# Splitting the first layer-norm block by tokens and moving the last tile's masks into the next tile

## The chip, the cores and the metric

The kernel runs on one core of one Trainium2 chip. The metric is the device time of one execution in microseconds; the time before is the median of three runs. The profile is of one further execution, with times counted from the start of its span.

## The reference

The reference is one step of a two-layer model on 384 tokens (128 context, 256 latent) of width D = 1024, in float32. Cut to the parts that matter here:

```python
def conv_module(h, pw1, dw, dw_b, ln_g, ln_b, pw2):
    a, g = jnp.split(h @ pw1, 2, axis=-1)
    u = a * jax.nn.sigmoid(g)
    u = depthwise_conv(u, dw) + dw_b            # 31 taps
    u = jax.nn.silu(layer_norm(u, ln_g, ln_b))
    return u @ pw2

def layer_norm(x, g, b):
    xc = x - mean(x)
    return xc * lax.rsqrt(mean(xc * xc) + EPS) * g + b

def moe_swiglu(h, w_router, w1, w3, w2):        # 8 experts, top 2
    out = 0
    for e in range(8):
        out = out + gates[:, e:e + 1] * ((silu(t @ w1[e]) * (t @ w3[e])) @ w2[e])
```

Layer 0 is the convolution module followed by a dense SwiGLU, layer 1 is latent attention followed by the eight experts. Each part is preceded by an RMS norm that a small linear map of the condition modulates.

## The kernel before, in words

Every product with a weight matrix is made in three TensorE passes, high times high, low times high and high times low (`mm3`, lines 277 to 279). So each weight chunk (1 MB, [128, 2048]) passes four stations. SyncE loads it into one of six slots of `raw` (`load`, line 240); ScalarE makes the high part `wh` (`make_hi`, line 255); VectorE makes the low part `wl` = raw − wh (`make_lo`, line 261); TensorE uses both. `wh` and `wl` have three slots each. A slot of `raw` is free once its low part is made, and a slot of `wh` and `wl` once TensorE has used the chunk. The order on each engine is written out by hand, one instruction stream an engine, tied by counting semaphores.

**Start of the convolution.** ScalarE modulates the normed input in eight blocks of 128 channels, and VectorE splits each block into `hTh` and `hTl` (`split_block`, lines 415 and 417). VectorE makes the low part of the first weight chunk, PW1, between the first split and the other seven. TensorE's first product needs that low part and the first split block, and each later one the next block.

**Layer norm of the convolution.** Channels lie on partitions, eight blocks `v[:, j, :]` of 399 columns: 128 context tokens, 15 columns of padding, 256 latent tokens. TensorE sums the squares over all channels with a matrix of ones into PSUM (line 1715). Then, once for all 399 columns: ScalarE takes the root into `sd` (line 749), VectorE the reciprocal `rs` (line 1130). For each block j VectorE scales by `rs` (line 1134), ScalarE applies Silu in two pieces of 128 and 256 tokens (line 753), and VectorE splits the result. Line 1136 splits block j − 2 after scaling block j. TensorE's product with `pw2` (`pw2_block`) waits for the split of block k and takes three groups of 128 tokens from it, of six passes each.

**Experts.** Tokens sorted by expert are handled in tiles of 128. Expert 0's first tile is gathered on the chip by a product with selection masks; its chunks are MOE to MOE+11 (six for w1, six for w3). GpSimd meanwhile writes all tokens to `xs_dram` with six indirect DMAs (line 660), and then makes the masks `selL` of the last tile (lines 667 to 678), which are needed only at the very end of the kernel. In the first tile, after its eighth chunk (MOE+7), TensorE waits for these masks, transposes them and makes six short passes for the gate weights (lines 2116 to 2122). ScalarE then copies `sel` and `selT` (lines 977 to 981) and VectorE copies `slot_w` (lines 1569 to 1573), each in order between two weight conversions.

After MOE+9 TensorE turns the rows of the second tile, `xrow` (line 2100). SyncE fetches them (line 521) when all six indirect DMAs have landed; until then it issues nothing else, since the next chunks stand behind that wait on its queue. The function `tile` then handles the chunks NEXT to NEXT+17 (NEXT = MOE+12) of the next tile: w1 six, w3 six, w2 six chunks. It is written once as a static call, `tile(0, static=True)`, and then runs in a loop.

Of the kernel before, what the change touches and what calls it, by code (L numbers as in the profile page):

```python
# [15 lines left out]
P = 128  # L16
# [37 lines left out]
def hybrid_conv_mla_diffusion_step(nc, d, out):  # L54
# [45 lines left out]
    POST_TAPS = (24, 30, 38)  # L100
    GATE_EARLY = 4
    TILE_CH = 6 * NG
    NEXT = MOE + 12
# [3 lines left out]
    with ctx:  # L107
# [88 lines left out]
        def sem(name):  # L196

            if name not in named:
                named[name] = ctx.enter_context(nc.semaphore(name))
            return named[name]  # L200
# [210 lines left out]

        def split_block(dve, q, made, per, j):

            dve.wait_ge(sem(made), per * (j + 1))
            dve.tensor_copy(hTh[:, j, :], hf[:, j, :]).then_inc(sem("h_hi"), 1)
            dve.wait_ge(sem("h_hi"), SPLITS.index(q) * DK + j + 1)
            dve.tensor_tensor(hTl[:, j, :], hf[:, j, :], hTh[:, j, :], ALU.subtract).then_inc(sem(q + "_h_lo"), 1)  # L417
# [13 lines left out]
        def _(sp):  # L431
# [91 lines left out]
            with sp.Fori(1, NE - 1) as e:  # L523
                load_next(e, e + 1, e)
            sp.wait_ge(sem("tab_ready"), 1)
            more = sp.value_load(tab[0:1, 0:1], min_val=0, max_val=NX)
# [13 lines left out]
        def _(pool):  # L540
# [124 lines left out]
            pool_step.n = 9  # L665
            pool.wait_ge(sem("weights_made"), 1)
            pool_step(pool.tensor_scalar(first, jt[:, 2, NE - 1:NE], float(NE - 1), float(P), ALU.add, ALU.mult))
# [23 lines left out]
        def _(act):  # L691
# [56 lines left out]
            act.wait_ge(sem("ln_summed"), DK)  # L748
            act.activation(sd, ps[:, 5, 0:CV], ACT.Sqrt, scale=1.0 / D, bias=epsc[:, 0:1]).then_inc(sem("ln_root"), 1)
            for j in range(DK):  # L750
                act.wait_ge(sem("ln_scaled"), j + 1)
                for a, b, o in ((0, P, 0), (P, T, SV - P)):
                    act.activation(hf[:, j, a:b], v[:, j, a + o:b + o], ACT.Silu, scale=vT[:, LNG + j:LNG + j + 1],
                                   bias=vT[:, LNB + j:LNB + j + 1]).then_inc(sem("ln_done"), 1)
# [155 lines left out]
            turned_k(0, turns())  # L910
            act.wait_ge(sem("first_turned"), 1)
            act.activation(KR[:, :], ps[:, 3, :], ACT.Copy).then_inc(sem("rT_made"), 1)
# [29 lines left out]
            token_scale(0)  # L942
            act.wait_ge(sem("x_turned"), 1)
            act.activation(yacc[:, 0, :], ps[:, X_BANKS[0]:X_BANKS[0] + 2, :].rearrange("p a b -> p (a b)"),
# [30 lines left out]
            for k in range(2 * UP - 1):  # L975
                make_hi(act, MOE + k + 3)
                if k == UP + 1:
                    act.wait_ge(sem("last_tile"), TC + 1)
                    for c in range(TC):
                        act.activation(sel[:, c, :], ident[:, :], ACT.Copy, scale=rt[:, 9, c, 3:4])  # L980
                    act.activation(selT[:, :], ps[:, 6, 0:T], ACT.Copy).then_inc(sem("last_tile"), 1)
                if k == UP:
                    silu(MOE + UP, None)
                if k == 2 * UP - 3:
                    rows_hi(xgh[:, :, :], (sem("xg_turned"), 1))
# [6 lines left out]
            def tile(e, static=False):  # L992

                L, L1, L3 = (None,) * 3 if static else ((e, TILE_CH), (e, 1), (e, 3))
                for k in range(-1, TILE_CH - 1):
                    make_hi(act, NEXT + k + 3, L)
                    if k in (1, 2, 3):
                        hidden_hi(k - 1, L3)
                    if k == 1 and not static:
                        store_y(ys_dram[ds(e * P - P, P), :], at(1, L1), sem("y_stored"))  # L1000
                    if k == UP:
                        act.wait_ge(sem("hm_made"), at(3, L3))
                        silu(NEXT + UP, L)
                    if k == 2 * UP + 2:
                        rows_hi(xgh[:, :, :], (sem("xg_turned"), at(2, L1)))
                act.wait_ge(chunk_used, at(NEXT + TILE_CH, L))
                if not static:
                    act.wait_ge(sem("y_stored"), at(0, (e, 16)))
                act.activation(ybuf[:, :], ps[:, 6:8, :].rearrange("p a b -> p (a b)"), ACT.Copy).then_inc(sem("y_copied"), 1)

            tile(0, static=True)
            with act.Fori(1, NE - 1) as e:
                tile(e)
            act.wait_ge(sem("tab_ready"), 1)
            more = act.value_load(tab[0:1, 0:1], min_val=0, max_val=NX)
# [14 lines left out]
        def _(dve):  # L1030
# [59 lines left out]
            modulation(0)  # L1090
            split_block(dve, "conv", "conv_modulated", 2, 0)
            make_lo(dve, PW1)
            for j in range(1, DK):
                split_block(dve, "conv", "conv_modulated", 2, j)
            dve.wait_ge(sem("zeroed"), 3)
# [31 lines left out]
            for q in range(2):  # L1127
                make_lo(dve, pw2_chunk(q))
            dve.wait_ge(sem("ln_root"), 1)
            step(dve.reciprocal(rs, sd))  # L1130
            dve.wait_ge(sem("ln_centred"), DK)
            for j in range(DK + 2):
                if j < DK:
                    dve.tensor_tensor(v[:, j, :], v[:, j, :], rs, ALU.mult).then_inc(sem("ln_scaled"), 1)
                if j >= 2:
                    split_block(dve, "ln", "ln_done", 2, j - 2)
            add_bias(4)
# [284 lines left out]
            for c in (1, 2):  # L1422
                dve.wait_ge(sem("x_turned"), c + 1)
                dve.tensor_copy(yacc[:, c, :], ps[:, X_BANKS[c]:X_BANKS[c] + 2, :].rearrange("p a b -> p (a b)")).then_inc(sem("router_made"), 1)
# [86 lines left out]
            def weights():  # L1511

                dve.wait_ge(sem("token_steps"), 3 * TC + 1)
                step(dve.tensor_scalar(gap[:, :, 2:3], gap[:, :, 1:2], 1.0, None, ALU.add))
                dve.reciprocal(gap[:, :, 3:4], gap[:, :, 2:3]).then_inc(sem("weights_made"), 1)

# [44 lines left out]
            for k in range(1, 2 * UP - 1):  # L1561
                if k == 2 * UP - 2:
                    product(MOE + 2 * UP, None, 1, groups=(0,))
                make_lo(dve, MOE + k + 3)
                if k == 2:
                    extra_tiles()
                if k == 4:
                    table()
                if k == UP + 1:
                    dve.wait_ge(sem("last_tile"), TC + 1)  # L1570
                    step(dve.tensor_copy(slot_w[:, :], ps[:, 7, 0:2]))
                    dve.wait_ge(sem("last_tile"), TC + 2)
                    dve.sem_inc(sem("y_copied"), 1)
                if k == 2 * UP - 3:
                    rows_lo(xgl[:, :, :], xgh[:, :, :], 0, (sem("xg_hi"), 1))
            product(MOE + 2 * UP, None, 1, groups=(1,))

            def tile(e, static=False):

                L, L1, L3 = (None,) * 3 if static else ((e, TILE_CH), (e, 1), (e, 3))  # L1580
                for k in range(-1, TILE_CH - 1):
# [3 lines left out]
                    if k in (1, 2, 3):  # L1585
                        hidden_lo(k - 1, L3)
                    if k == 2 * UP:
                        product(NEXT + 2 * UP, L, at(2, L1), (sem("hm_turned"), at(3, L3)))
# [36 lines left out]
        def _(pe):  # L1625
# [94 lines left out]
            def pw2_block(q, i, c, hi, lo):  # L1720

                k = 2 * q + i
                pe.wait_ge(sem("ln_h_lo"), k + 1)
                for h in range(2):
# [4 lines left out]

            pe.wait_ge(sem("ln_root"), 1)  # L1730
            for q in range(DK // 2):
# [273 lines left out]
            for c in range(KC):  # L2005
                last = pe.transpose(ps[:, 3, c * P:(c + 1) * P], krh[:, c, :, :].rearrange("p a b -> p (a b)"), ident[:, :])
            last.then_inc(sem("first_turned"), 1)
            pe.wait_ge(sem("q_copied"), 1)
# [105 lines left out]
            for i in range(UP):  # L2114
                up_chunk(MOE + UP, i, 3, hgh, hgl, None)
                if i == 1:
                    pe.wait_ge(sem("last_tile"), TC)
                    for c in range(TC):
                        pe.transpose(ps[:, 6, c * P:(c + 1) * P], selL[:, c, :], ident[:, :])
                    for c in range(TC):  # L2120
                        last = pe.matmul(ps[:, 7, 0:2], selL[:, c, :], GL[:, c, :], start=c == 0, stop=c == TC - 1)
                    last.then_inc(sem("last_tile"), 1)
                if i == UP - 3:
                    turn_rows_in(1, 16)

            def tile(e, static=False):
# [8 lines left out]
                for i in range(UP):  # L2135
                    up_chunk(NEXT + UP, i, 3, xgh, xgl, L)
                pe.wait_ge(sem("y_copied"), at(1, L1))
                for i in range(2 * NG):
# [5 lines left out]
            with pe.Fori(1, NE - 1) as e:  # L2144
                tile(e)
            pe.wait_ge(sem("tab_ready"), 1)
            more = pe.value_load(tab[0:1, 0:1], min_val=0, max_val=NX)
# [77 lines left out]
```

## Time and profile before

| | |
|---|---|
| runs before, median (lowest to highest) | 1447.17 us (1446.88 to 1450.38) |
| the profiled execution, its own time | 1447.64 us |
| its span | 1445.9 us |
| mean granted TensorE clock | 0.978 of full speed |
| TensorE busy | 1369.8 us, 95% |
| VectorE busy | 1060.7 us, 73% |
| ScalarE busy | 756.3 us, 52% |
| GpSimd busy | 100.6 us, 7% |
| bytes moved by DMA | 351 MB, 243 GB/s over the span |

The execution's own time is 1.7 us above its span and 0.5 us above the median of the runs. Busy times of different engines overlap. In the rows below, PE is TensorE, PEld its weight load, DVE is VectorE, ACT is ScalarE, POOL is GpSimd and SPq SyncE's DMA issues. L1130 is line 1130 of the kernel before.

### The profile page before, as it was taken

What the parts mean: (1) busy time and instruction counts of PE and PEld (TensorE: products, weight loads), DVE (VectorE), ACT (ScalarE), POOL (GpSimd) and SP (SyncE); (2) the same over time, 40 slices, a digit from 0 to 9 for tenths busy, and PEclk for the clock granted to TensorE, in tenths of its full rate; (3) what the DMA queues carried; (4) which work ended last, traced back from release to release, by engine and by line L of the source; (5) the groups of instructions that cost most, each with busy time, mean ns of one, the idle gap of its engine ahead of it and who ended that gap; (6) DMA issues with size and microseconds to landing.
All of it is one profiled execution on the core that took longest, in us unless ns stands there. A gap on an engine that the chain in (4) does not pass through costs nothing.

```text
span 1445.9 us, 18716 instructions
## 1 busy us (share of the span) xinstructions
PE 1369.8 (95%) x6687; PEld 1100.4 (76%) x6687; DVE 1060.7 (73%) x1328; ACT 756.3 (52%) x764; POOL 100.6 (7%) x129
## 2 busy tenths in 40 slices
PE   4999989999999989899999978799999999999997
PEld 1885456999999978677777757587878878878875
DVE  1689985443433457888888889588888888888986
ACT  2431355222312255655555545577777777777773
POOL 2000000401000001100000015200000000000003
PEclk8999999999999989999999998899999999999999
DMA  9898556989743324322222235799999999999994
GB/s 376 293 339 322 204 203 225 400 337 64 198 145 103 122 50 128 104 66 66 79 80 87 89 116 206 301 375 375 363 385 380 364 363 395 369 362 381 385 361 152
DMA packets 91914, 351.17 MB, mean 243 GB/s; under 512 B 7279, under 2 KB 43447, under 8 KB 62679
## 3 DMA queue, kind: packets, MB, share of 16 engines
q1 hardware_dynamic: 81088, 316.95, 61.4%
q0 software_dynamic: 9040, 28.66, 5.8%
q10 hardware_dynamic: 1735, 4.89, 0.8%
q8 instruction: 30, 0.49, 0.1%
q14 instruction: 21, 0.17, 0.0%
HBM read 326.13 MB, written 24.35 MB: 242 GB/s over the span
## 4 chain that ended last, share of the span: by engine, by line
PE 81%; DVE 8%; ACT 3%; issue 3%; POOL 2%; DMA 1%; ACTq 0%; DVEq 0%
PE ps L277 23%; PE ps L279 22%; PE ps L278 22%; PE ps L1699 3%; PE ps L1644 3%; DVE wl L261 2%; DVE hm L1551 2%; PE ps L1945 2%; DMA raw<-in_conv_pw 1%; PE ps L1976 1%; ACT wh L255 1%; PE ps L1949 1%; POOL xs_dram L660 1%; PE ps L2107 1%; ACT QB L850 0%
## 5 line engine op out<-in xcount | busy, mean ns | idle before, releaser
L261 DVE TENSOR_TENSOR wl<-raw,wh 128x2048 fp32r<-128x2048 f32 x253 | 575.9, 2290 | 151.8 <-ACT wh L255 151.6
L255 ACT ACTIVATE wh<-raw 128x2048 fp32r<-128x2048 f32 x253 | 484.1, 1917 | 306.0 <-PE ps L279 267.4
L277 PE MATMUL ps<-wh,xgh 128*128 128x512 f32 x432 | 173.5, 402 | 0.1
L279 PE MATMUL ps<-wh,xgl 128*128 128x512 f32 x432 | 171.1, 396 | 0.0
L278 PE MATMUL ps<-wl,xgh 128*128 128x512 f32 x432 | 171.0, 396 | 0.0
L277 PE MATMUL ps<-hTh,wh 128*128 128x384 f32 x480 | 164.7, 343 | 1.8 <-DVE hTl L417 1.8
L278 PE MATMUL ps<-hTl,wh 128*128 128x384 f32 x480 | 163.3, 340 | 0.0
L279 PE MATMUL ps<-hTh,wl 128*128 128x384 f32 x480 | 163.0, 340 | 0.0
L277 PE MATMUL ps<-wh,hgh 128*128 128x512 f32 x288 | 118.2, 410 | 3.6 <-DVE hgl L1557 1.9
L278 PE MATMUL ps<-wl,hgh 128*128 128x512 f32 x288 | 115.8, 402 | 0.0
L279 PE MATMUL ps<-wh,hgl 128*128 128x512 f32 x288 | 115.6, 402 | 0.0
L1072 DVE SCALAR_TENSOR_TENSOR v<-u,dwT,v 128x399 f32<-128x399 f32 x180 | 99.1, 639 | 0.0
L277 PEld LDWEIGHTS ps<-hTh,wh 128*128 128x128 f32 x480 | 90.5, 189 | 10.8 <-issue 7.9
L1158 DVE TENSOR_TENSOR ff<-ps,fs 128x384 f32<-128x384 f32 x22 | 12.3, 558 | 114.9 <-PE ps L279 114.9
L279 PEld LDWEIGHTS ps<-wh,xgl 128*128 128x128 f32 x432 | 81.4, 188 | 19.8
L277 PEld LDWEIGHTS ps<-wh,xgh 128*128 128x128 f32 x432 | 81.4, 188 | 19.1 <-DVE wl L261 0.4
L278 PEld LDWEIGHTS ps<-wl,xgh 128*128 128x128 f32 x432 | 81.4, 188 | 18.3
L278 PEld LDWEIGHTS ps<-hTl,wh 128*128 128x128 f32 x480 | 90.7, 189 | 0.4
L279 PEld LDWEIGHTS ps<-hTh,wl 128*128 128x128 f32 x480 | 90.6, 189 | 0.0
L277 PEld LDWEIGHTS ps<-wh,hgh 128*128 128x128 f32 x288 | 55.2, 192 | 20.8 <-DVE wl L261 5.5
L279 PEld LDWEIGHTS ps<-wh,hgl 128*128 128x128 f32 x288 | 55.3, 192 | 13.6
L278 PEld LDWEIGHTS ps<-wl,hgh 128*128 128x128 f32 x288 | 55.4, 192 | 12.5
(368 smaller groups left out, 2122.7 us busy)
## 6 DMA issues: line engine op xcount, KB each, us to landing
raw<-in_moe_w SPq DMA_DIRECT2D x180, 1024.0 KB, 6.1
raw<-in_ada_w SPq DMA_DIRECT2D x48, 1024.0 KB, 6.6
raw<-in_ffn_w SPq DMA_DIRECT2D x33, 1024.0 KB, 11.5
raw<-in_conv_pw SPq DMA_DIRECT2D x12, 1024.0 KB, 9.2
raw<-in_mla_wo SPq DMA_DIRECT2D x8, 1024.0 KB, 4.8
xs_dram<-hf POOLq DMA_DIRECT2D x14, 512.0 KB, 21.2
ys_dram<-hf POOLq DMA_DIRECT2D x14, 512.0 KB, 22.3
raw<-in_mla_wuq SPq DMA_DIRECT2D x8, 768.0 KB, 4.6
```

Source lines behind the costliest of these rows:

```text
L255: act.activation(wh[:, split_no(s) % HL, :], raw[:, s % RAW, :], ACT.Copy).then_inc(hi_made, 1)
L261: eng.tensor_tensor(wl[:, split_no(s) % HL, :], raw[:, s % RAW, :], wh[:, split_no(s) % HL, :], ALU.subtract).then_inc(lo_made, 1)
L277: nc.tensor.matmul(out_, sh, mh, start=start, stop=False)
L278: nc.tensor.matmul(out_, sh, ml, start=False, stop=False)
L279: return nc.tensor.matmul(out_, sl, mh, start=False, stop=stop)
L660: pool.indirect_dma_start(out=xs_dram[:, :], out_offset=bass.IndirectOffsetOnAxis(ap=rows_of[:, c, i:i + 1], axis=0), in_=xn[:, c, :], in_ ...
L1072: dve.scalar_tensor_tensor(out=v[:, j, :], in0=u[:, j, w:w + CV], scalar=dwT[:, w * DK + j:w * DK + j + 1], in1=v[:, j, :], op0=ALU.mult, ...
L1551: dve.tensor_tensor(hm[:, g, :].rearrange("p (j r) -> p r j", j=4), ps[:, 3 + g, :].rearrange("p (r j) -> p r j", j=4), ms[:, g, :].rearra ...
L1644: last = pe.matmul(ps[32 * j:32 * j + 32, ADA_BANKS[q][0], :], cst[:, k, :], raw[:, s % RAW, j * 512:(j + 1) * 512], start=k == 0, stop=k ...
L1699: pe.matmul(ps[:, i, 0:CV], diag[:, m % DIAGS, :], u[:, DVE_BLOCKS + i, w:w + CV], start=w == 0, stop=w == CW - 1).then_inc(sem("diag_used ...
L1945: pe.matmul(ps[:, 2 * h + c // 2, a:b], QB[:, h, c * P:(c + 1) * P], KT[:, h, k0:k1], start=True, stop=False)
L1949: last = pe.matmul(ps[:, 2 * h + c // 2, a:b], QB[r0:r1, 2, c * P:(c + 1) * P], KR[r0:r1, k0:k1], start=False, stop=True)
```

## The change

The change has three parts and a renaming.

1. **Layer norm.** The 399 columns are cut in three parts, `LN_PARTS`: columns 0 to 128, 128 to 271 and 271 to 399, which hold the three groups of 128 tokens. Root and reciprocal are made for each part. For block 0, scaling, Silu and the split are made by part as well, and TensorE's first product waits for one part at a time. Blocks 1 to 7 stay as they were, with the split of block j − 2 behind the scaling of block j.
2. **Masks of the last tile.** The wait for `selL`, the transposes and short passes on TensorE, the copies on ScalarE and VectorE move from the first tile (behind MOE+7 on TensorE) into the static `tile(0)`: behind NEXT+7 on TensorE, behind the conversions of NEXT+11 on ScalarE and VectorE.
3. **Start of the convolution.** VectorE makes the low part of PW1 ahead of all eight splits.
4. Two semaphores that were used once, `first_turned` and `weights_made`, become the first count of `x_turned` and `tab_ready`; the later counts are one higher.

```diff
+    LN_PARTS = ((0, P, 0), (P, SV + P, P), (SV + P, CV, 2 * P))
@@ split_block
-            dve.wait_ge(sem(made), per * (j + 1))
+            dve.wait_ge(sem(made), per * (j + 1) + more)
@@ ScalarE, layer norm
-            act.activation(sd, ps[:, 5, 0:CV], ACT.Sqrt, scale=1.0 / D, bias=epsc[:, 0:1]).then_inc(sem("ln_root"), 1)
-            for j in range(DK):
-                act.wait_ge(sem("ln_scaled"), j + 1)
+            for a, b, _ in LN_PARTS:
+                act.activation(sd[:, a:b], ps[:, 5, a:b], ACT.Sqrt, scale=1.0 / D, bias=epsc[:, 0:1]).then_inc(sem("ln_root"), 1)
+            for i, (_, b, o) in enumerate(LN_PARTS):
+                act.wait_ge(sem("ln_scaled"), i + 1)
+                act.activation(hf[:, 0, o:o + P], v[:, 0, b - P:b], ACT.Silu, scale=vT[:, LNG:LNG + 1],
+                               bias=vT[:, LNB:LNB + 1]).then_inc(sem("ln_done"), 1)
+            for j in range(1, DK):
+                act.wait_ge(sem("ln_scaled"), TC + j)
@@ ScalarE, first tile of the experts
-                if k == UP + 1:
-                    act.wait_ge(sem("last_tile"), TC + 1)
-                    for c in range(TC):
-                        act.activation(sel[:, c, :], ident[:, :], ACT.Copy, scale=rt[:, 9, c, 3:4])
-                    act.activation(selT[:, :], ps[:, 6, 0:T], ACT.Copy).then_inc(sem("last_tile"), 1)
@@ ScalarE, tile: the same five lines
+                    if static and k == UP + 2:
...
@@ VectorE, start of the convolution
-            split_block(dve, "conv", "conv_modulated", 2, 0)
             make_lo(dve, PW1)
-            for j in range(1, DK):
-                split_block(dve, "conv", "conv_modulated", 2, j)
+            split_dve(dve, "conv", "conv_modulated", 2)
@@ VectorE, layer norm
-            dve.wait_ge(sem("ln_root"), 1)
-            step(dve.reciprocal(rs, sd))
             dve.wait_ge(sem("ln_centred"), DK)
-            for j in range(DK + 2):
+            for i in range(TC + 1):
+                if i < TC:
+                    a, b, _ = LN_PARTS[i]
+                    dve.wait_ge(sem("ln_root"), i + 1)
+                    step(dve.reciprocal(rs[:, a:b], sd[:, a:b]))
+                if i > 0:
+                    o = LN_PARTS[i - 1][2]
+                    dve.wait_ge(sem("ln_done"), i)
+                    high = dve.tensor_copy(hTh[:, 0, o:o + P], hf[:, 0, o:o + P])
+                    if i < TC:
+                        step(high)
+                    else:
+                        high.then_inc(sem("h_hi"), 1)
+                        dve.wait_ge(sem("h_hi"), SPLITS.index("ln") * DK + 1)
+                    dve.tensor_tensor(hTl[:, 0, o:o + P], hf[:, 0, o:o + P], hTh[:, 0, o:o + P], ALU.subtract)\
+                        .then_inc(sem("ln_h_lo"), 1)
+                if i < TC:
+                    dve.tensor_tensor(v[:, 0, a:b], v[:, 0, a:b], rs[:, a:b], ALU.mult).then_inc(sem("ln_scaled"), 1)
+            for j in range(1, DK + 2):
                 if j < DK:
                     dve.tensor_tensor(v[:, j, :], v[:, j, :], rs, ALU.mult).then_inc(sem("ln_scaled"), 1)
-                if j >= 2:
-                    split_block(dve, "ln", "ln_done", 2, j - 2)
+                if j >= 3:
+                    split_block(dve, "ln", "ln_done", 2, j - 2, 1)
@@ VectorE, first tile of the experts
-                if k == UP + 1:
-                    dve.wait_ge(sem("last_tile"), TC + 1)
-                    step(dve.tensor_copy(slot_w[:, :], ps[:, 7, 0:2]))
-                    dve.wait_ge(sem("last_tile"), TC + 2)
-                    dve.sem_inc(sem("y_copied"), 1)
@@ VectorE, tile: the same four lines
+                    if static and k == UP + 2:
...
@@ TensorE, product with pw2
-                pe.wait_ge(sem("ln_h_lo"), k + 1)
+                pe.wait_ge(sem("ln_h_lo"), c + 1 if k == 0 else TC + k)
...
-            pe.wait_ge(sem("ln_root"), 1)
+            pe.wait_ge(sem("ln_root"), TC)
@@ TensorE, first tile of the experts
                 up_chunk(MOE + UP, i, 3, hgh, hgl, None)
-                if i == 1:
-                    pe.wait_ge(sem("last_tile"), TC)
-                    for c in range(TC):
-                        pe.transpose(ps[:, 6, c * P:(c + 1) * P], selL[:, c, :], ident[:, :])
-                    for c in range(TC):
-                        last = pe.matmul(ps[:, 7, 0:2], selL[:, c, :], GL[:, c, :], start=c == 0, stop=c == TC - 1)
-                    last.then_inc(sem("last_tile"), 1)
@@ TensorE, tile: the same six lines
                     up_chunk(NEXT + UP, i, 3, xgh, xgl, L)
+                    if static and i == 1:
...
```

## Rows read from the trace of the kernel before

**Rows 1.** The page: busy time, and the costliest groups of instructions (mean ns of one).

```profile
PE 1369.8 (95%) x6687; PEld 1100.4 (76%) x6687; DVE 1060.7 (73%) x1328; ACT 756.3 (52%) x764; POOL 100.6 (7%) x129
...
L261 DVE TENSOR_TENSOR wl<-raw,wh 128x2048 fp32r<-128x2048 f32 x253 | 575.9, 2290 | 151.8 <-ACT wh L255 151.6
L255 ACT ACTIVATE wh<-raw 128x2048 fp32r<-128x2048 f32 x253 | 484.1, 1917 | 306.0 <-PE ps L279 267.4
```

**Rows 2.** Waits of PE over the span: us in total, times, longest us.

```profile
PE ps L2119 <- POOL selL L678: 9.0, 1, 9.0
PE ps L277 <- DVE hTl L417: 7.8, 3, 3.7
```

**Rows 3.** Timeline of the layer norm: start us, us, engine, line, operation [idle before].

```profile
194.19 1.28 ACT L749 ACT_TABLE_LOAD   x1
...
195.48 0.60 ACT L749 ACTIVATE sg<-ps,epsc 128x399 f32<-128x399 f32 x1
...
196.10 1.28 ACT L753 ACT_TABLE_LOAD   x1
196.11 2.65 DVE L1130 RECIPROCAL sg<-sg 128x399 f32<-128x399 f32 x1 [0.30 <-ACT sg L749]
...
199.41 3.61 ACT L753 ACTIVATE hf<-v,vT 128x128 f32<-128x128 f32 x8 [2.03 <-DVE v L1134]
...
201.52 0.77 PE L277 MATMUL ps<-wh,hTh 128*128 128x512 f32 x1 [3.65 <-DVE hTl L417]
```

**Rows 4.** Groups with shapes kept apart, DVE and ACT: busy us, mean ns.

```profile
L415 DVE CAST hTh<-hf 128x384 fp32r<-128x384 f32 x32 | 11.4, 356 | 9.9 <-ACT hf L348 8.5 <-ACT hf L321 1.2
...
L1325 DVE RECIPROCAL st<-st 128x4 f32<-128x4 f32 x8 | 1.4, 179 | 4.4 <-ACT pr L884 4.4
...
L1217 DVE TENSOR_TENSOR qr<-ckv,pT 128x128 f32<-128x128 f32 x2 | 0.6, 292 | 0.1
...
L753 ACT ACTIVATE hf<-v,vT 128x128 f32<-128x128 f32 x8 | 3.9, 488 | 3.3 <-DVE v L1134 3.3
```

**Rows 5.** Stretches: length, busy by engine, granted clock, DMA share, GB/s.

```profile
201.50:205.00 3.50, 3.48 (x8) 2.81 (x9) 3.40 (x9) 2.91 (x8) 0.00 (x0) 0.51 1.10 357
205.00:237.00 32.00, 32.00 (x140) 25.78 (x139) 18.09 (x22) 12.78 (x15) 1.08 (x2) 1.00 0.58 205
...
915.70:921.20 5.50, 5.50 (x14) 4.34 (x14) 0.16 (x1) 1.39 (x5) 0.00 (x0) 0.50 1.01 425
...
984.00:1037.00 53.00, 52.86 (x238) 42.47 (x236) 46.33 (x26) 39.01 (x24) 0.00 (x0) 1.00 0.97 375
```

**Rows 6.** Timeline of the start: the first weight load of the first product.

```profile
37.34 0.28 PEld L277 LDWEIGHTS ps<-hTh,wh 128*128 128x128 f32 x1 [0.27 <-DVE wl L261]
```

**Rows 7.** Timeline of PE around the masks.

```profile
913.77 0.90 PE L2119 MATMUL ps<-ident,selL 128*128 128x128 f32 x3 [8.96 <-POOL selL L678]
...
930.57 0.39 PE L277 MATMUL ps<-wh,xgh 128*128 128x512 f32 x1
...
934.12 0.50 PE L277 MATMUL ps<-wh,xgh 128*128 128x512 f32 x1
```

**Rows 8.** Timeline of POOL: the first and the last of the nine mask instructions.

```profile
904.12 2.71 POOL L676 TENSOR_SCALAR selL<-iota,off 128x128 f32<-128x128 f32 x1
...
913.26 0.45 POOL L678 TENSOR_TENSOR selL<-selL,before 128x128 f32<-128x128 f32 x1
```

**Rows 9.** Timeline of SPq: the issues that follow its wait for the indirect DMAs.

```profile
907.71 0.33 SPq L521 DMA_DIRECT2D xrow<-xs_dram  x1
908.13 17.68 SPq L240 DMA_DIRECT2D raw<-in_moe_w  x6
```

**Rows 10.** DMA issues from 908.0 to 908.6: count, KB, us to landing.

```profile
raw<-in_moe_w SPq DMA_DIRECT2D x1, 1024.0 KB, 5.9
xrow<-xs_dram SPq DMA_DIRECT2D x1, 512.0 KB, 3.5
```

**Rows 11.** DMA rate from 880 to 935 in 40 slices of 1.375 us.

```profile
GB/s 0 0 354 27 119 280 328 366 432 420 429 426 423 429 423 420 417 429 372 24 30 265 426 447 387 447 411 441 417 435 423 72 0 83 244 402 420 435 310 24
```

More of the change, by code:

```diff
@@ L410, in split_dve, with split_block @@
                 split_block(dve, q, made, per, j)
-        def split_block(dve, q, made, per, j):
-            dve.wait_ge(sem(made), per * (j + 1))
+        def split_block(dve, q, made, per, j, more=0):
+            dve.wait_ge(sem(made), per * (j + 1) + more)
             dve.tensor_copy(hTh[:, j, :], hf[:, j, :]).then_inc(sem("h_hi"), 1)
@@ L524, in _ @@
                 load_next(e, e + 1, e)
-            sp.wait_ge(sem("tab_ready"), 1)
+            sp.wait_ge(sem("tab_ready"), 2)
             more = sp.value_load(tab[0:1, 0:1], min_val=0, max_val=NX)
@@ L665, in _ @@
             pool_step.n = 9
-            pool.wait_ge(sem("weights_made"), 1)
+            pool.wait_ge(sem("tab_ready"), 1)
             pool_step(pool.tensor_scalar(first, jt[:, 2, NE - 1:NE], float(NE - 1), float(P), ALU.add, ALU.mult))
@@ L910, in _ @@
             turned_k(0, turns())
-            act.wait_ge(sem("first_turned"), 1)
+            act.wait_ge(sem("x_turned"), 1)
             act.activation(KR[:, :], ps[:, 3, :], ACT.Copy).then_inc(sem("rT_made"), 1)
@@ L942, in _ @@
             token_scale(0)
-            act.wait_ge(sem("x_turned"), 1)
+            act.wait_ge(sem("x_turned"), 2)
             act.activation(yacc[:, 0, :], ps[:, X_BANKS[0]:X_BANKS[0] + 2, :].rearrange("p a b -> p (a b)"),
@@ L1003, in tile @@
                         silu(NEXT + UP, L)
+                    if static and k == UP + 2:
+                        act.wait_ge(sem("last_tile"), TC + 1)
+                        for c in range(TC):
+                            act.activation(sel[:, c, :], ident[:, :], ACT.Copy, scale=rt[:, 9, c, 3:4])
+                        act.activation(selT[:, :], ps[:, 6, 0:T], ACT.Copy).then_inc(sem("last_tile"), 1)
                     if k == 2 * UP + 2:
@@ L1013, in _ @@
                 tile(e)
-            act.wait_ge(sem("tab_ready"), 1)
+            act.wait_ge(sem("tab_ready"), 2)
             more = act.value_load(tab[0:1, 0:1], min_val=0, max_val=NX)
@@ L1422, in _ @@
             for c in (1, 2):
-                dve.wait_ge(sem("x_turned"), c + 1)
+                dve.wait_ge(sem("x_turned"), c + 2)
                 dve.tensor_copy(yacc[:, c, :], ps[:, X_BANKS[c]:X_BANKS[c] + 2, :].rearrange("p a b -> p (a b)")).then_inc(sem("router_made"), 1)
@@ L1514, in weights @@
                 step(dve.tensor_scalar(gap[:, :, 2:3], gap[:, :, 1:2], 1.0, None, ALU.add))
-                dve.reciprocal(gap[:, :, 3:4], gap[:, :, 2:3]).then_inc(sem("weights_made"), 1)
+                dve.reciprocal(gap[:, :, 3:4], gap[:, :, 2:3]).then_inc(sem("tab_ready"), 1)
             has, to, w = xj[:, 0, :, :], xj[:, 1, :, :], xj[:, 2, :, :]
@@ L1586, in tile @@
                         hidden_lo(k - 1, L3)
+                    if static and k == UP + 2:
+                        dve.wait_ge(sem("last_tile"), TC + 1)
+                        step(dve.tensor_copy(slot_w[:, :], ps[:, 7, 0:2]))
+                        dve.wait_ge(sem("last_tile"), TC + 2)
+                        dve.sem_inc(sem("y_copied"), 1)
                     if k == 2 * UP:
@@ L2006, in _ @@
                 last = pe.transpose(ps[:, 3, c * P:(c + 1) * P], krh[:, c, :, :].rearrange("p a b -> p (a b)"), ident[:, :])
-            last.then_inc(sem("first_turned"), 1)
+            last.then_inc(sem("x_turned"), 1)
             pe.wait_ge(sem("q_copied"), 1)
@@ L2136, in tile @@
                     up_chunk(NEXT + UP, i, 3, xgh, xgl, L)
+                    if static and i == 1:
+                        pe.wait_ge(sem("last_tile"), TC)
+                        for c in range(TC):
+                            pe.transpose(ps[:, 6, c * P:(c + 1) * P], selL[:, c, :], ident[:, :])
+                        for c in range(TC):
+                            last = pe.matmul(ps[:, 7, 0:2], selL[:, c, :], GL[:, c, :], start=c == 0, stop=c == TC - 1)
+                        last.then_inc(sem("last_tile"), 1)
                 pe.wait_ge(sem("y_copied"), at(1, L1))
@@ L2145, in _ @@
                 tile(e)
-            pe.wait_ge(sem("tab_ready"), 1)
+            pe.wait_ge(sem("tab_ready"), 2)
             more = pe.value_load(tab[0:1, 0:1], min_val=0, max_val=NX)
```

## The prediction

> **What bounds the kernel now.** I read the page first. TensorE is busy for 1369.8 of 1445.9 us [rows 1], so time can only come from the other 76 us or from stretches at the lower clock. The list of PE's waits shows where they lie: the longest single one is 9.0 us at the transposes of the last tile's masks, ended by GpSimd, and another of 3.7 us stands before the first product with `pw2` [rows 2]. The change touches both places. The table of stretches adds what a stop costs afterwards. Behind each of the two the granted clock is 0.51 and 0.50, the 1.2 GHz level: 8 passes took 3.5 us and 14 took 5.5 us, 0.43 and 0.39 us each, where 140 passes at full clock (2.4 GHz) took 32.0 us, 0.23 us each [rows 5]. A chunk of 12 passes is thus 2.8 us at full clock.
>
> **Masks, what goes.** Before, TensorE ended MOE+7 at 913.77 − 8.96 = 904.8, and began the next tile's first chunk, NEXT, at 930.57 and NEXT+1 at 934.12 [rows 7]. Without the masks it does MOE+8 and MOE+9 to 904.8 + 5.6 = 910.4. Then a wait takes the old one's place: `xrow` was issued at 907.71 [rows 9] and landed 3.5 us later [rows 10], at 911.2. SyncE is released by GpSimd's indirect DMAs, whose order is untouched, so this time stays. Eight transposes of some 0.11 us (0.9 us) end at 912.1, MOE+10 and MOE+11 at 917.7. NEXT needs more: its weights were issued at 908.13 and take 5.9 us [rows 9, 10], to 914.0. High part 1.92 us and low part 2.29 us [rows 1] bring 918.2; the low part of the rows, 128 x 1024 on VectorE right behind it, adds 1.1. So NEXT begins at 919.3 instead of 930.57, after a second stop of 1.6 us: 11.2 us earlier. NEXT+1 was held by its low part, 3.55 us after NEXT. Now its weights land about 2.5 us behind the first (1 MB at 420 GB/s [rows 11]), at 916.5; with the product of the hidden group ahead of it, VectorE ends that low part at 922.4, when TensorE comes from NEXT and four transposes at 922.6. That gives back another 0.3.
>
> **Masks, what comes.** In `tile(0)` three transposes and six short passes stand behind NEXT+7. At the low clock they lay between 913.77 and about 915.7, 1.9 us [rows 5, 7]; nine instructions at the 0.11 us of the other transposes are 1.0. The clock should be full there, so 1.0, with 1.9 as the other end. ScalarE's four copies are part of 1.39 us [rows 5] and VectorE's copy is 0.16. What hides them: ScalarE converts in 1.92 and VectorE in 2.29 of each 2.9 us that a chunk takes TensorE (52.9 us for 18 [rows 1, 5]). A high part delayed by 0.6 us still leaves its low part ready 0.8 us before TensorE needs it. If that cover failed, the cost would be 0.6, once. Neither waits there: the conversions of NEXT+11 start only when NEXT+8 is used, and that is behind the masks. Nothing is queued on SyncE behind the moved steps, but its issues shift: slots of `raw` are freed earlier, so the second `xrow` and NEXT+6 follow the six queued chunks directly. NEXT+6 lands near 914.0 + 6 x 2.5 + 1.3 = 930.3, and ScalarE wants it at 931.9. **Sum of this part:** 11.2 + 0.3 − 1.0 = 10.5 us.
>
> **Layer norm.** Before: root 0.60, reciprocal 2.65, scaling, first Silu pair from 199.41, high and low part of the block, TensorE at 201.52 [rows 3]. Now, first part (128 columns). Root: between its share of 0.60 (0.19) and the 0.49 of a Silu of that width [rows 4]; I take 0.39 (nearest in width), ready 195.9. Reciprocal: 4 columns took 0.18 and 399 took 2.65 [rows 3, 4], so 6.26 ns a column, 0.96 for 128; ready 196.85. Scaling 0.29 [rows 4], 197.2. But ScalarE does two more roots (0.33 apart) ahead of the Silu table load, which begins at 196.57, not 196.10, and ends at 197.85. So the table load, not VectorE, sets the first Silu: 197.87 to 198.36. Meanwhile VectorE takes the second reciprocal (143 columns, 1.05). High part 0.2 (a third of 0.36 is 0.12, plus its fixed share), low part 0.29: ready 198.9, TensorE at 199.05, 2.5 us earlier. By the same durations part two is ready at 200.7 and part three at 202.0; block 1, behind three full scalings, at 204.35.
>
> Here the clock decides how TensorE uses this. Its stop shrinks from 3.65 us to 1.2. If the clock stays full, each part takes 1.4 us, and block 1 starts when VectorE has it, 204.35. Before, block 1 started after 8 slow and 10 fast passes, at 207.35. The gain is 3.0. If the clock falls all the same, 8 slow passes to 202.6 and 10 fast end at 204.95: gain 2.4. I take 2.9, being nearer to the first, as the stop is a third of the old one. The cover behind this is wide: a block takes TensorE 4.2 us and VectorE 1.5. The three extra instructions on each of root, reciprocal and scaling cost nothing more for that reason.
>
> Before, a load of a table was followed by the next activation at once: load 194.19 to 195.47, root at 195.48 [rows 3]. The Trainium skill (ScalarE: Activation LUTs, What ACT_TABLE_LOAD costs) gives a switch about 1.38 us of drain beside its 1.28. By that rule the first Silu would come at about 199.2 and the layer norm would gain 1.6, not 2.9. The row shows no such drain for the root's load, so the sum keeps 2.9.
>
> **Start.** TensorE's weight load sat idle 0.27 us for the low part of PW1 [rows 6]; that part can start 1.7 us earlier. The transposes before it end at about 37.2, so the gain is between 0 and 0.27; I take 0.1. The splits come later than before only for block 0. The renamed semaphores cost nothing: nobody waits for the counts that moved out of turn.
>
> **Sum.** 10.5 + 2.9 + 0.1 = 13.5 from the profiled execution's 1447.64: 1434.1. It lies 0.5 above the median of the runs, so 1434.0 is said for the new median, between 1433.7 and 1434.1. Both gains pass on to the end, since no stretch after them shows a wait of TensorE for a DMA.
>
> **Rivals.**
> *The weight stream is the bound (0.10).* For: while tiles run, the DMA share is 0.97 at 375 GB/s [rows 5]. After the change TensorE follows the restart at 908.13 closely, and what the stream cannot catch up is lost. Before, it had a pause around 922 to 928, when the slots were full: slices of 72, 0, 83 and 244 GB/s against 420 [rows 11], worth 4.2 us. If 375 is all it can do in tiles, only this pause is won: 1447.6 − 4.2 − 3.0 = 1440.4, and with no pause won 1444.6. Against: the same queues gave 411 to 447 GB/s just before the pause [rows 11], and weights landed 5.9 us after issue, far less than six slots' worth of 17 us. The Trainium skill (SBUF — State Buffer, a bandwidth intuition that's wrong) gives about 358 GB/s of memory to a core and calls it the usual bound; rates of 375 and over here exceed it.
>
> *The clock falls at the short stops (0.08).* The stops of 0.8 and 1.6 us before NEXT may bring the low level, as 9.0 did; 14 slow passes cost 14 x 0.16 to 0.20 = 2.2 to 2.7 us: 1436.5. Against: each is under half of the 3.65 us stop.
>
> *The layer norm gains nothing (0.05).* Each part goes ScalarE, VectorE, ScalarE, VectorE; a root that ended at 196.08 released the reciprocal at 196.11 [rows 3], 0.03 us. If handing over cost 0.3 instead (the idle time of [rows 6]) in the eight places up to block 1, 2.2 of the 2.9 would go: 1436.2. Against: the hand-over that rows 3 show is the same kind.
>
> *The masks come late (0.02, the slower side).* GpSimd's mask instruction took 2.71 us at 904.12 beside a low-part conversion, the last one 0.45 [rows 8]. The SBUF page of the Trainium skill has a port pair shared by VectorE and GpSimd, locked for a whole instruction; the trace agrees. Now conversions never pause, so one mask instruction may pass a chunk: nine end at 904.1 + 9 x 2.8 = 929.3. TensorE asks at about 943, which is the deciding point. Were only every second gap caught, they would end at 954.5: 11.5 us of wait and 2.7 at the low clock, 1448.3, slower than before; at every third gap they end near 980.
>
> **Chances.** The forecast has 0.75, with an own range of 1432.3 to 1436.0 from the ends above (0.9 more for masks, 0.5 less and 1.3 more in the layer norm, 0.7 for landings). The range 1431.8 to 1437.8 takes in two rivals and leaves out the stream and the late masks. 0.3% (4.3 us) is what a measurement of this kernel can tell. Faster by more: 0.95; within: 0.04 (a full stream, or masks late by every second gap); slower: 0.01 (masks later still).
>
> **What would show it.** Right: no wait of PE for `selL`; a wait of about 0.8 us before line 2100's transposes and 1 to 2 us before NEXT; NEXT 26 − 11.2 = 14.6 us after MOE+7; granted clock 1.0 there; first `pw2` pass 2.5 us earlier, block 1 about 3.0. Wrong: PE waiting in `tile(0)` for weights (stream), clock at 0.5 near either stop, or a wait for `selL` behind NEXT+7.

## The result, and the profile after

| | before | changed |
|---|---|---|
| median of the runs (lowest to highest), same chip | 1447.07 us (1446.51 to 1450.38), 6 runs | 1439.84 us (1437.10 to 1441.74), 6 runs |
| ratio of all runs' times, 95% interval | | 0.9945 [0.9932, 0.9957] |
| profiled execution: own time, span | 1447.64, 1445.9 | 1441.74, 1440.0 |
| mean granted TensorE clock | 0.978 | 0.977 |

The change makes the kernel faster by 7.2 us by the medians (0.5%). The forecast was 1434.0, which is 13.2 under the 1447.17 it started from, and 1439.84 lies outside its range of 1431.8 to 1437.8. The sign was right, and about half the gain is missing. The profiled execution of the changed kernel is the slowest of its six, 1.9 us above their median, and its mean clock of 0.977 the lowest; the other five show 0.981 to 0.983. What its trace shows of the clock below is therefore the upper end of these runs, not their middle.

The busy times of the page, against [rows 1], have hardly moved:

```profile
PE 1373.4 (95%) x6686; PEld 1102.0 (77%) x6687; DVE 1061.3 (74%) x1336; ACT 756.7 (53%) x767; POOL 104.5 (7%) x129
```

PE's waits over the span are the view that answers to [rows 2] (us in total, times, longest us):

```profile
PE ps L278 <- DVE hTl L418: 4.9, 3, 2.3
...
PE ps L1672 <- DVE ar L1048: 4.1, 2, 3.2
...
PE ps L278 <- DVE hTl L1148: 1.1, 1, 1.1
```

The 9.0 us for `selL` are gone. The 3.7 us before the first product with `pw2` have become 1.1. But a wait that did not stand among the long ones has come in: 3.2 us at line 1672, which is no product with a weight. It is `turn_rows`, four transposes that turn a row of the modulation of the next layers into columns; the row is `ar`, to which VectorE adds the bias on line 1048 (`add_bias(4)`). In TensorE's order it stands behind the first `pw2` chunk, blocks 0 and 1.

The timeline of the layer norm, changed kernel (columns as in [rows 3]), first ScalarE and VectorE:

```profile
195.58 0.90 ACT L751 ACTIVATE sg<-ps,epsc 128x128 f32<-128x128 f32 x3
196.05 0.95 DVE L1138 RECIPROCAL sg<-sg 128x128 f32<-128x128 f32 x1
196.50 1.28 ACT L754 ACT_TABLE_LOAD   x1
...
197.79 0.49 ACT L754 ACTIVATE hf<-v,vT 128x128 f32<-128x128 f32 x1
...
203.47 0.36 DVE L416 CAST hTh<-hf 128x384 fp32r<-128x384 f32 x1
...
211.45 0.68 DVE L1048 TENSOR_TENSOR ar<-ps,ab 128x512 f32<-128x512 f32 x1
```

and TensorE:

```profile
199.09 0.47 PE L278 MATMUL ps<-wh,hTh 128*128 128x512 f32 x1 [1.11 <-DVE hTl L1148]
...
200.66 0.50 PE L278 MATMUL ps<-wh,hTh 128*128 128x512 f32 x1
...
204.47 0.51 PE L278 MATMUL ps<-wh,hTh 128*128 128x512 f32 x1 [0.74 <-DVE hTl L418]
...
212.19 1.11 PE L1672 MATMUL ps<-ident,ar 128*128 128x128 f32 x4 [3.24 <-DVE ar L1048]
212.96 0.78 PE L278 MATMUL ps<-wh,hTh 128*128 128x512 f32 x1
```

The same three instructions in the kernel before, the split of block 1, the bias and the turning, not shown ahead of the prediction:

```profile
201.78 0.36 DVE L415 CAST hTh<-hf 128x384 fp32r<-128x384 f32 x1
...
209.76 0.68 DVE L1042 TENSOR_TENSOR ar<-ps,ab 128x512 f32<-128x512 f32 x1
...
211.57 0.60 PE L1652 MATMUL ps<-ident,ar 128*128 128x128 f32 x4
```

What the reader is to see: the first products start where the prediction put them, 199.09 and 204.47 against 199.05 and 204.35. TensorE then comes to the turning at 212.19 − 3.24 = 208.95, which is 2.6 us earlier than before. The bias comes 1.7 us later than before (211.45 against 209.76), because VectorE works off block 0 in parts first, the split of block 1 begins 1.7 later (203.47 against 201.78), and the bias stands behind all eight splits on VectorE. Before, the bias was done at 210.44 and TensorE needed it at 211.57, a margin of 1.1 us. 2.6 + 1.7 − 1.1 = 3.2 us, the wait in the row. So TensorE goes on 0.6 us later than before rather than 3 earlier, and in this execution it then runs at the low clock. The stretches (columns as in [rows 5]):

```profile
204.40:208.80 4.40, 4.33 (x18) 3.31 (x18) 4.30 (x11) 3.65 (x8) 0.00 (x0) 1.00 1.10 399
208.80:212.20 3.40, 0.16 (x2) 0.01 (x1) 3.30 (x9) 3.22 (x4) 0.00 (x0) 0.81 0.75 313
212.20:217.40 5.20, 5.20 (x15) 4.23 (x16) 4.48 (x4) 1.37 (x1) 1.08 (x2) 0.50 0.39 118
217.40:237.00 19.60, 19.60 (x85) 15.76 (x84) 5.02 (x3) 5.32 (x4) 0.00 (x0) 0.99 0.35 132
```

The clock stayed at its high level behind the stop of 1.1 us, as forecast, and fell to the 1.2 GHz level behind the new one of 3.2 us. By the end of the `pw2` products the changed kernel is 3.2 us later than the one before: the same VectorE instruction starts at 225.84 in it and at 222.65 before.

### The profile page after: what moved, and what is told of

Its sections match the earlier page's. It is cut to its first block, busy times and chain, and to the rows that moved or that the text cites. A ratio compares the mean times of both kernels' runs of the same rounds, so it can differ in the third digit from the quotient of the medians.

```text
span 1440.0 us, 18728 instructions
## 1 busy us (share of the span) xinstructions
PE 1373.4 (95%) x6686; PEld 1102.0 (77%) x6687; DVE 1061.3 (74%) x1336; ACT 756.7 (53%) x767; POOL 104.5 (7%) x129
## 4 chain that ended last, share of the span: by engine, by line
PE 81%; DVE 9%; issue 4%; ACT 4%; DMA 2%; SPq 0%; POOL 0%; DVEq 0%; ACTq 0%; POOLq 0%
PE ps L278 23%; PE ps L280 22%; PE ps L279 22%; PE ps L1719 3%; PE ps L1664 2%; DVE wl L262 2%; DVE hm L1571 2%; PE ps L1965 2%; PE ps L1996 2%; DMA raw<-in_ada_w 1%; ACT wh L256 1%; PE ps L1969 1%; PE ps L2127 1%; PE ps L2086 1%; ACT QB L856 0%
## 5 line engine op out<-in xcount | busy, mean ns | idle before, releaser
L278 PEld LDWEIGHTS ps<-hTh,wh 128*128 128x128 f32 x480 | 90.5, 188 | 10.5 <-issue 7.9
## 6 DMA issues: line engine op xcount, KB each, us to landing
raw<-in_ffn_w SPq DMA_DIRECT2D x33, 1024.0 KB, 12.5
```

What stands on the lines that cost most here:

```text
L278: nc.tensor.matmul(out_, sh, mh, start=start, stop=False)
```

## The experiments

Each ratio below compares a version's runs with runs of the kernel before on the same chip. The theory: the masks are worth what was forecast, and the gain of the layer norm is lost, and more, in the wait for the bias. The rivals: the weight stream or a clock lost at the short stops eats part of the masks' gain; or the missing time is the layer norm's own, in its hand-overs or its extra instructions.

**Masks alone.** Part 2 and the renaming on the kernel before; start and layer norm as they were.

```diff
@@ TensorE (and the like on ScalarE and VectorE)
             for i in range(UP):
                 up_chunk(MOE + UP, i, 3, hgh, hgl, None)
-                if i == 1:
-                    ...
@@ tile
                     up_chunk(NEXT + UP, i, 3, xgh, xgl, L)
+                    if static and i == 1:
+                        ...
```

> The kernel before with the masks moved alone. Theory A (the masks' part works as predicted or better; the shortfall of the whole change lies in the layer norm): 9 to 13 us below before, 1434 to 1438. Rival B (the weight stream holds TensorE back behind the moved masks): 3 to 6 us below, 1441 to 1444. In the profile A wants PE's wait for xrow at 0.8 us or none and the next tile's first pass about 11 us earlier than in the kernel before.

Measured: 1436.88 us (1436.42 to 1437.80) against 1447.37, ratio 0.9925 [0.9912, 0.9939]. The medians are 10.5 us apart, the sum of this part to a tenth. The timeline of TensorE in this run:

```profile
911.12 1.06 PE L2101 MATMUL ps<-ident,xrow 128*128 128x128 f32 x8 [1.14 <-DMA xrow<-xs_dram]
...
919.02 0.50 PE L278 MATMUL ps<-wh,xgh 128*128 128x512 f32 x1 [1.23 <-DVE xgl L1542]
...
922.29 0.48 PE L278 MATMUL ps<-wh,xgh 128*128 128x512 f32 x1
...
942.88 0.49 PE L2134 MATMUL ps<-ident,selL 128*128 128x128 f32 x3
943.21 0.73 PE L2136 MATMUL ps<-GL,selL 128*128 128x2 f32 x6
```

and its stretches behind the restart:

```profile
911.10:919.00 7.90, 6.67 (x32) 5.25 (x32) 5.03 (x4) 5.01 (x4) 4.05 (x5) 1.00 1.01 423
919.00:930.00 11.00, 10.98 (x54) 9.00 (x55) 11.00 (x7) 7.21 (x5) 0.00 (x0) 1.00 1.02 422
930.00:983.00 53.00, 52.91 (x242) 42.67 (x241) 46.08 (x27) 39.13 (x29) 0.00 (x0) 1.00 0.98 391
```

911.2, 919.3, 922.6 and 943 were forecast for the four; the stops are 1.1 and 1.2 us and the clock is 1.00 behind both. The weight stream did 422 GB/s while it caught up and 391 after, so TensorE stayed busy for 52.91 of 53 us. The stream is no bound at 375 GB/s, and the clock did not fall at these stops in this execution; the five runs lie within 1.4 us of each other and none lacks the gain. Both rivals are out.

**Layer norm alone.** Part 1 and the renaming on the kernel before; masks and start as they were.

> The kernel before with the layer norm's split by parts alone. Theory A: TensorE reaches the turning of the modulation rows (turn_rows(4), behind the second pw2 block) 3 us earlier than VectorE has added their bias, waits 3.2 us there, and goes on at the low clock: 2 to 4 us slower than before, 1449 to 1451. Rival C (the gain of 3 us at block 1 is kept, something later lost it in the whole change): 2 to 3 us faster, 1444 to 1445.

Measured: 1449.19 us (1447.26 to 1452.61, 11 runs) against 1447.37, ratio 1.0013 [1.0004, 1.0022]. Alone, the part of which 2.9 us were forecast makes the kernel slower by 1.8. Its list of PE's waits between 195 and 240, and two stretches:

```profile
PE ps L1674 <- DVE ar L1048: 3.2, 1, 3.2
```

```profile
208.50:212.00 3.50, 0.26 (x2) 0.12 (x2) 3.40 (x9) 3.33 (x4) 0.00 (x0) 1.00 0.75 311
212.00:217.40 5.40, 5.40 (x26) 4.43 (x27) 4.38 (x4) 1.26 (x1) 1.08 (x2) 1.00 0.44 135
```

The wait is there with the same length, but in this execution the clock did not fall behind it: 26 passes in 5.4 us, not 15 in 5.2. The VectorE instruction that stands at 222.65 before stands at 223.02 here, 0.4 later. So a cancelled gain is what the wait costs with the clock kept. That the execution as a whole took 1447.68 us, beside 1447.64 before, is partly chance: it lost 1.6 us more at a fall of the clock near 248, 1.7 near 881, and won 3.3 back in the stage with the wait for `selL`, which is 7.2 us long here and not 9.0 (the table of delays below). The median lies 1.5 above this execution. The mean clocks of the runs fit falls of the clock in the others, 0.981 to 0.982 in the three fastest and 0.973 to 0.980 in the other eight, but no profile of those was taken, so where it fell in them is not shown.

**Turning later, in the changed kernel.** If the wait is the cause, the turning need only stand behind the second `pw2` chunk, where the bias has long been made. What it turns is needed only after all four chunks.

```diff
-                if q == 0:
+                if q == 1:
                     turn_rows(4)
```

> The changed kernel with turn_rows(4) behind the second chunk of pw2 instead of the first. Theory A: the wait of 3.2 us and the low clock behind it (2.1 us) go, so 5 to 6.5 us below the changed kernel, 1433.5 to 1435 against 1439.8. Rival C (what was lost lies elsewhere): within 1 us of the changed kernel.

Measured: 1434.92 us (1433.64 to 1435.87), ratio 0.991 [0.9897, 0.9924]. That is 4.9 below the median of the changed kernel, or 5.2 when each is held against its own runs of before (12.5 against 7.2), and 0.9 above the forecast of 1434.0. The turning now waits for nothing:

```profile
217.08 0.60 PE L1672 MATMUL ps<-ident,ar 128*128 128x128 f32 x4
```

**Turning later, with the layer norm alone.** The same edit on the kernel of the second experiment.

> The kernel before with the layer norm's split by parts and turn_rows(4) behind the second chunk of pw2; no masks moved. Theory A: the predicted gain of the layer norm shows by itself, 2.5 to 3.5 us below before, 1443.5 to 1444.5. Rival C: no gain, 1447. Rival D (where the clock falls in later stretches depends on the exact arrival, and shifts of 3 us cost or give as much): anything from 1442 to 1448 with a spread of runs over 2 us.

Measured: 1444.93 us (1443.52 to 1446.31, 11 runs) against 1447.37, ratio 0.9981 [0.9972, 0.9990]: 2.4 us faster than before, where 2.9 was forecast for the layer norm, and 4.3 faster than without the edit. The gain exists, so the hand-overs and the extra instructions do not eat it; it lies 0.1 under the lower end that theory A gave. Rival D is not out: the runs spread over 2.8 us, and in the profiled execution the clock did fall later on, 0.74 from 540 to 545 and again near 878. But the 21 runs of the kernel before spread over 4.4 us, so the spread does not single D out; D explains the noise and not the 4.3 us.

**Turning later, in the kernel before: the control.** The edit might be a gain of its own.

> A control: the kernel before with turn_rows(4) behind the second chunk of pw2 and nothing else. Theory A (the move only helps where TensorE comes too early): TensorE did not wait there before, so within 1 us of the kernel before, 1446.5 to 1448. Rival E (the place behind the second chunk is better in itself, and the layer norm's split brings nothing): 2 to 3 us faster, 1444.5 to 1445.5.

Measured: 1447.79 us (1447.19 to 1449.82, 11 runs) against 1447.00 for the kernel before on the same chip, ratio 1.0004 [0.9996, 1.0013]. No gain. The edit gives something only where the layer norm is split.

**Bias earlier.** The other way to take the wait away: VectorE adds the bias between the splits of blocks 3 and 4, and TensorE's order stays as it was.

```diff
                 if j >= 3:
                     split_block(dve, "ln", "ln_done", 2, j - 2, 1)
-            add_bias(4)
+                if j == 5:
+                    add_bias(4)
```

> The changed kernel with VectorE's add_bias(4) moved from behind all eight blocks' splits to behind the split of block 3; TensorE's order untouched. Theory A (the wait is for the bias, which stands behind the splits): wait gone, 1434 to 1436, as with turn_rows(4) moved. Rival F (TensorE's time behind the first chunk matters, not VectorE's order): no better than 1439.

Measured: 1434.41 us (1433.47 to 1434.79) against 1447.00, ratio 0.9909 [0.9895, 0.9924], 12.6 us faster than before and with "turning later" the fastest version of this study; the two ratios can't be told apart. Its timeline and its stretch:

```profile
206.63 0.68 DVE L1048 TENSOR_TENSOR ar<-ps,ab 128x512 f32<-128x512 f32 x1
...
208.39 0.60 PE L1673 MATMUL ps<-ident,ar 128*128 128x128 f32 x4
```

```profile
204.40:217.40 13.00, 13.00 (x59) 10.51 (x58) 11.76 (x21) 7.84 (x11) 1.09 (x2) 1.00 0.70 255
```

The bias is made 4.8 us earlier, TensorE turns it when it gets there, and is busy for all of 13.0 us at full clock. The VectorE instruction that stood at 222.31 in the run with the masks alone stands at 219.46 here, 2.85 us earlier: the layer norm's gain of 2.9 at this place. Of this, 2.1 us are left at the end by the medians (12.6 against 10.5), and the next table shows where this execution lost some. One edit moves TensorE's step and the other VectorE's; both end in the same place, which, with the control, leaves the wait between the two as the cause.

**Start alone.** Part 3 on the kernel before.

> The kernel before with the low part of PW1 ahead of all eight splits, nothing else. Forecast: 0.1 us faster, not to be told from the kernel before (1447 to 1447.6). Rival G (later splits hold the first product back): 0.5 to 1 us slower.

Measured: 1447.48 us (1445.59 to 1450.97, 12 runs) against 1447.00, ratio 1.0006 [0.9998, 1.0015]: no difference that these runs resolve, as 0.1 us has to look. The first product begins at 37.33 in this run and at 37.35 before.

## Why the prediction was wrong, point by point

**Masks: right.** In the run with the masks alone, no wait for `selL`, the two short stops, the restart and the price of the masks in `tile(0)` (the nine instructions took 1.0 us at full clock) came as worked out, and 10.5 us by the medians with this part alone. GpSimd's masks ended at 915.4 there and at 923.0 in the changed kernel; TensorE asks at 942.88 there and at 948.24 in the changed kernel, so they were never late. The mechanism of the rival is there, though: GpSimd, changed kernel, one mask instruction held beside low-part conversions:

```profile
916.03 4.76 POOL L678 TENSOR_SCALAR before<-iota,off 128x128 f32<-128x128 f32 x1
920.88 2.15 POOL L679 TENSOR_TENSOR selL<-selL,before 128x128 f32<-128x128 f32 x1
```

**Layer norm up to block 1: right.** The table load began at 196.50 (196.57 forecast), the first Silu followed its end of 197.78 at once, at 197.79, and no drain of 1.38 us showed, as the row of before had said. Hand-overs were as short as assumed. The clock stayed full over the stop of 1.1.

**Start: of no weight.** The first product comes 0.02 us earlier, of a forecast 0.1, and the runs can't resolve either.

**The step that failed** is "The cover behind this is wide: a block takes TensorE 4.2 us and VectorE 1.5", with what was built on it, "cost nothing more for that reason" and "Both gains pass on to the end". The comparison was right for the blocks and left out what stands between them on TensorE. The queue is block 0, block 1, turning, block 2; the turning needs not the next block but the bias, which is VectorE's last step behind all eight splits. For it the cover is not 4.2 against 1.5 but the 1.1 us of margin before. The forecast and the trace of before held the numbers against it: block 1 ready at 204.35 is 1.6 us later than VectorE had it before, and everything behind it on VectorE is as late, while TensorE was to come 3.0 earlier. 1.6 + 3.0 against 1.1 was a wait of 3.5 us, and 3.24 came. In place of the gain of 2.9, this part costs 1.8 us by the medians, from the wait and, where it falls, the clock. No rival had this place; the one called "The layer norm gains nothing" looked for the loss in the hand-overs, which were right.

**What the parts add up to.** By the medians of the parts alone, −10.5 + 1.8 + 0.5 = −8.2 against −7.2 measured, with the start's 0.5 not to be told from nought. The 1.0 between them is not resolved: the changed kernel's six runs spread over 4.6 us, those of before over 3.9. With the turning later the parts do add up: −10.5 − 2.4 + 0.5 = −12.4 against −12.5.

In the profiled executions the time is not lost in one piece. The table gives how much later (+) or earlier (−) than in the kernel before the same low part of a weight chunk starts on VectorE, in us; the columns are the starts in the kernel before.

| | 231 | 272 | 557 | 887 | 1425 |
|---|---|---|---|---|---|
| changed kernel | +3.2 | +3.2 | +4.5 | +7.3 | −5.6 |
| masks alone | −0.3 | −0.3 | −0.4 | −0.5 | −10.9 |
| layer norm alone | +0.4 | +1.9 | +2.1 | +3.7 | +0.4 |
| changed, turning later | −2.9 | −2.9 | −3.1 | −3.1 | −13.6 |
| changed, bias earlier | −3.2 | −1.6 | −1.4 | +0.2 | −12.7 |
| before, turning later (control) | +1.3 | +1.3 | +1.3 | +3.9 | +0.7 |

Each step up to the right of 231 is a stretch that ran at a lower clock than before, at a place that no edit touches and not in every execution. The control's +1.3 is of the same kind: behind the 3.65 us stop that it shares with the kernel before, its clock stayed low for longer (10 passes from 205 to 208, where before there are 14). Near 248, behind a stop of 1.8 us that all nine executions have, it fell with the bias earlier and with the layer norm alone, and held in the other seven. Bias earlier and turning later:

```profile
245.00:248.00 3.00, 3.00 (x12) 2.90 (x12) 1.57 (x4) 1.32 (x4) 0.00 (x0) 0.50 1.10 360
```

```profile
245.00:248.00 3.00, 3.00 (x21) 2.93 (x21) 2.30 (x7) 1.93 (x5) 0.00 (x0) 1.00 1.08 364
```

Near 545 it was low in the changed kernel (the first line) and not before:

```profile
543.00:548.00 5.00, 5.00 (x21) 4.96 (x20) 4.90 (x8) 1.88 (x5) 0.00 (x0) 0.50 0.01 3
```

```profile
543.00:548.00 5.00, 5.00 (x38) 4.98 (x37) 3.63 (x7) 2.74 (x7) 0.00 (x0) 1.00 0.41 129
```

Near 880 the 32 gathering passes of the experts' first tile took 3.82 us before, 5.65 in the changed kernel and 5.57 in the control, which has no part of the change:

```profile
877.44 3.82 PE L2066 MATMUL ps<-sel,xn 128*128 128x128 f32 x32
```

```profile
882.92 5.65 PE L2086 MATMUL ps<-sel,xn 128*128 128x128 f32 x32
```

```profile
879.61 5.57 PE L2066 MATMUL ps<-sel,xn 128*128 128x128 f32 x32
```

What decides where the clock falls in an execution stays open.

In the changed kernel the experts' first chunk begins 7.3 us late. The stage that begins there then wins 12.8 us rather than the masks' 10.5, and with the bias earlier, where the clock fell near 880 too, it does the same. The surplus is time caught up at a wait that stood there anyway: `xrow` was issued at the same time as before, 907.85 against 907.71 [rows 9], although the stage began 7.3 us later. TensorE came to it at 917.57 and found the rows landed, so both short stops were gone. Changed kernel, SyncE and TensorE:

```profile
907.85 0.33 SPq L522 DMA_DIRECT2D xrow<-xs_dram  x1
...
917.57 1.03 PE L2120 MATMUL ps<-ident,xrow 128*128 128x128 f32 x8
...
924.06 0.39 PE L278 MATMUL ps<-wh,xgh 128*128 128x512 f32 x1
```

What is lost ahead of such a wait comes back in part at the wait. The two stops were 2.4 us together with the masks alone. 7.3 − 12.8 is the −5.5 us that this execution shows at its end.

## What to carry to other kernels

When a stage of one engine is sped up, list what stands behind it in the engine's own order, short steps above all, and look up for each who makes its input and where that stands in the maker's order. A margin in the trace of before, the time by which an input was ready too early, is the most that the change may take on both sides together. Here 1.1 us of margin met a TensorE 2.6 us earlier and a VectorE 1.7 us later. Where a split in parts makes the splitting engine busier at the front, move its small late duties ahead of the last blocks, or their users behind.

## What the runs showed of the hardware

- The same stop at the same place can cost the clock or not. The 3.24 us stop left it at 0.50 for 5.2 us in one execution (changed kernel) and at 1.00 in another (layer norm alone). Behind the 1.8 us stop near 245 it fell in two of nine executions. The 1.1 us stop before the first product with `pw2` did not bring the low level in any of the five executions that have it. So one trace shows one draw: before a gain or loss of 1 to 3 us is put down to an edit, look whether the stretches that the edit does not touch ran at the same clock.
- The 128 x 128 comparison on line 678 of GpSimd took 0.61 us at 914.21 and 4.76 us at 916.03 in the changed kernel; beside the first VectorE stood idle, beside the second it made low parts without a pause. An indirect DMA's issue on GpSimd took 2.97 us at 882.70 in the kernel before and 0.98 us at 888.18 in the changed one. `xrow` waits for six of these, and its issue came between 900.79 (bias earlier) and 907.85 (changed kernel) with the same order on GpSimd. In bias earlier TensorE reached the rows at 910.44, 0.5 us later than with the masks alone, found them landed, and began NEXT at 916.93 instead of 919.02. So the two stops that the forecast counted as lost, 2.4 us, are a reserve in which some lateness of the stages ahead disappears.
